# Reordering and re-splitting the work between two token groups at the start of three matmul phases (dsa_shortconv_adaln_hybrid_step)

## The reference, cut to what matters

```python
def rms_norm(x, g):
    xf = x.astype(jnp.float32)
    y = xf * lax.rsqrt(jnp.mean(xf * xf, axis=-1, keepdims=True) + EPS)
    return y.astype(x.dtype) * g
...
def swiglu(h, w_gu, w_down):
    g, u = jnp.split(h @ w_gu, 2, axis=-1)
    return (jax.nn.silu(g) * u) @ w_down
...
        hp = rms_norm(yp, norm2_g[i]) * (1.0 + sc2p) + sh2p
        hs = rms_norm(ys, norm2_g[i]) * (1.0 + sc2s) + sh2s
        yp = yp + g2p * swiglu(hp, ffn_w_gu[i], ffn_w_down[i])
```

## Time and profile before

| | us |
|---|---|
| runs of the kernel before | 2651.3, 2657.64, 2664.18 (median 2657.64) |
| profiled execution, its own time | 2652.49 |
| profiled execution, span | 2650.6 |
| PE busy | 2514.7 (95%) |
| DVE busy | 1758.2 (66%) |
| POOL busy | 1274.7 (48%) |
| ACT busy | 1125.5 (42%) |

### The profile page before, as it was taken

One profiled execution on the slowest core, in us unless ns is written; L12 is line 12 of the kernel. 1 busy time (PEld: TensorE's weight loads), 2 busy tenths in 40 slices (PEclk: granted clock), 3 DMA queues, 4 the chain that ended last, 5 costly groups with the idle time before them and its releaser, 6 DMA issues.

```text
span 2650.6 us, 51647 instructions
## 1 busy us (share of the span) xinstructions
PE 2514.7 (95%) x20164; PEld 2315.4 (87%) x20164; DVE 1758.2 (66%) x3095; ACT 1125.5 (42%) x2073; POOL 1274.7 (48%) x967
## 2 busy tenths in 40 slices
PE   6979999999998999999999989999979999999999
PEld 4848864677898999999999989999979999999999
DVE  6498888665256665657667767766675666656775
ACT  5155656775245444444212453332454444442223
POOL 3403653343143656556545435545345656654444
PEclk7999999999999999999999999999999999999999
DMA  9215557102333434344985233338324434359731
GB/s 321 77 24 161 178 205 257 52 1 86 115 111 97 155 122 155 130 154 154 343 302 196 83 97 106 106 97 324 103 76 150 155 118 159 130 201 363 285 137 70
DMA packets 316389, 407.99 MB, mean 154 GB/s; under 512 B 40816, under 2 KB 227032, under 8 KB 313338
## 3 DMA queue, kind: packets, MB, share of 16 engines
q1 hardware_dynamic: 316154, 404.75, 45.6%
HBM read 284.85 MB, written 119.85 MB: 153 GB/s over the span
## 4 chain that ended last, share of the span: by engine, by line
PE 69%; DVE 12%; DMA 6%; issue 4%; POOL 4%; ACT 2%; SPq 2%; DVEq 0%; ACTq 0%; POOLq 0%
PE PS L595 9%; PE PS L2476 9%; PE PS L2478 9%; PE PS L2477 9%; PE PS L2533 5%; PE PS L2535 5%; PE PS L2536 5%; PE PS L1841 3%; PE PS L1870 2%; PE PS L1852 2%; DMA t_scratch<-stage 2%; POOL ring L2838 2%; DMA a_scratch<-stage 2%; POOL stage L2851 1%; DVE s_all L1538 1%
## 5 line engine op out<-in xcount | busy, mean ns | idle before, releaser
L2476 PE MATMUL PS<-th,ring 128*128 128x264 f32 x2800 | 802.9, 287 | 27.9 <-DVE y L3040 9.3
L2478 PE MATMUL PS<-th,ring 128*128 128x264 f32 x2800 | 798.8, 285 | 0.0
L2477 PE MATMUL PS<-th,ring 128*128 128x264 f32 x2800 | 797.9, 285 | 0.0
L2476 PEld LDWEIGHTS PS<-th,ring 128*128 128x128 f32 x2800 | 529.8, 189 | 35.6 <-issue 31.8
L2477 PEld LDWEIGHTS PS<-th,ring 128*128 128x128 f32 x2800 | 530.2, 189 | 0.0
L2478 PEld LDWEIGHTS PS<-th,ring 128*128 128x128 f32 x2800 | 529.9, 189 | 0.0
L2838 POOL TENSOR_TENSOR ring<-wraw,ring 128x512 fp32r<-128x512 f32 x232 | 333.7, 1441 | 396.1 <-ACT ring L2628 395.5
L2838 POOL TENSOR_TENSOR ring<-sums,ring 128x512 fp32r<-128x512 f32 x216 | 320.8, 1487 | 278.0 <-ACT ring L2628 277.9
L2533 PE MATMUL PS<-th,ring 128*128 128x264 f32 x1232 | 353.1, 287 | 16.5 <-DVE zs L3149 6.9
L2535 PE MATMUL PS<-th,ring 128*128 128x264 f32 x1232 | 351.7, 285 | 0.0
L2536 PE MATMUL PS<-th,ring 128*128 128x264 f32 x1232 | 351.2, 285 | 0.0
(11 more groups left out here) (387 smaller groups left out, 5179.7 us busy)
## 6 DMA issues: line engine op xcount, KB each, us to landing
t_scratch<-stage SPq DMA_DIRECT2D x154, 528.0 KB, 3.2
th<-t_scratch SPq DMA_DIRECT2D x77, 1056.0 KB, 8.6
wraw<-in_ffn_w_gu_dram SPq DMA_DIRECT2D x96, 512.0 KB, 5.2
wraw<-in_ada_w_dram SPq DMA_DIRECT2D x80, 512.0 KB, 4.8
wraw<-in_ffn_w_down_dram SPq DMA_DIRECT2D x80, 256.0 KB, 6.0
wraw<-in_conv_w_in_dram SPq DMA_DIRECT2D x28, 512.0 KB, 5.2
y<-y_scratch SPq DMA_DIRECT2D x12, 1056.0 KB, 8.8
y_scratch<-y SPq DMA_DIRECT2D x6, 2112.0 KB, 8.1
```

The source lines that it names most:

```text
L2476: pe.matmul(out, hi, x[:, TH, k, :], start=(k == 0 and i in (1, 2, 5)), stop=False, skip_group_check=True)
L2477: pe.matmul(out, hi, x[:, TL, k, :], start=False, stop=False, skip_group_check=True)
L2478: last = pe.matmul(out, lo, x[:, TH, k, :], start=False, stop=(k == 3), skip_group_check=True)
```

## The change

1. The scale is taken in `dve_row`: one SCALAR_TENSOR_TENSOR (y times the scale, times 1/rms) in place of a TENSOR_TENSOR. `act_row` is one ACTIVATE in place of two: it adds the shift while it rounds to the high part. The value in `xf` no longer has the shift. `dve_low_row` is a SCALAR_TENSOR_TENSOR that adds the shift and takes off the high part.
2. The token sums are made of rows without shift. In sums 5 and 4 the shifts cancel. In 6 and 7 a shift stays that differs by row, so their high part is four ACTIVATEs of 264 columns (one for each row) in place of one of 1056, and their low part four SCALAR_TENSOR_TENSORs in place of one TENSOR_TENSOR.
3. Setup: the shift of the samples is stored less that of the prompt (`dve_sample_shift`, three times), and three small differences of shifts go to `vec_g`.
4. Group 0's token sums stand now in g0 and u0, and the mean and the reciprocal of group 1 stand among them. Group 0's sum 7 is rounded in g1.
5. u0 and u1 run in halves: rows 0 to 3 of both tiles, then rows 4 to 7 of both, so weight slots come free in another order. `act_c_item` is rewritten: the rows of group 1 stand between the weight splits of u0 and at the head of g1.
6. The diagonal matrix of group 1 lies in `t12` instead of `rs2`. In the Z item ahead of phases 1 and 2 the reciprocal of group 0 and its broadcast come one unit earlier.

```diff
-                if _stage == "C" and _kind in "gc":
-                    DONE[-1] = _res + 1 + _pos // 2 if _pos % 2 else None
+                if _stage == "C" and _pos % 2 == 0:
+                    DONE[-1] = None
...
-            for mi, ft in side_by_side() if fresh else itertools.product(range(2), range(KT)):
+            for mi, ft in side_by_side() if fresh else by_halves():
...
-                elif fresh and (mi, ft) == (1, 3):
+                elif (mi, ft) == (1, 3):
                     last.then_inc(c_mm, 1)
...
         def act_c_item(act, it):
 
-            step = 2 * (it.kind in "uh") + 4 * it.groups[0]
+            f, split = it.phase, lambda pos: act_split(act, PREP_AT[it.n, pos])
             if it.kind in "gc":
-                for mi in range(2):
-                    act_split(act, PREP_AT[it.n, mi])
-                    act_c_take(act, it, mi)
-                act_c_build(act, it.phase, step)
-                act_c_build(act, it.phase, step + 1)
-                for pos in (2, 3):
-                    act_split(act, PREP_AT[it.n, pos])
+                if it.groups[0]:
+                    for ft in range(4, KT):
+                        act_row(act, f, 1, ft)
+                split(0)
+                if it.groups[0]:
+                    act_high_sum(act, f, 0, 7)
+                act_c_take(act, it, 0)
+                split(1)
+                act_c_take(act, it, 1)
+                act_high_sum(act, f, it.groups[0], 6)
+                if it.groups[0] == 0:
+                    act_root(act, f, 1)
+                act_high_sum(act, f, it.groups[0], 5)
+                split(2)
+                split(3)
                 return
...
+            act_high_sum(act, f, it.groups[0], 4)
+            for pos in range(4):
+                split(pos)
+                if it.groups[0] == 0 and pos in (1, 2):
+                    act_row(act, f, 1, 2 * pos - 2)
+                    act_row(act, f, 1, 2 * pos - 1)
...
-            act.activation(row[:, 0:w], row[:, 0:w], ACT.Identity, bias=part(lay, pt, ft)[:, 0:1], scale=gsc[:, f + 1, ft, 0:1])\
-                .then_inc(n_af, 1)
-            act.wait_ge(n_af, n)
-            at = (T_AT[1], T_AT[2])[b]
-            act.activation(th[s][:, TH, at:at + 2, k, :], row.rearrange("p (h n) -> p h n", h=2), ACT.Copy).then_inc(n_hi, 1)
+            act.activation(th[s][:, TH, at:at + 2, k, :], norm_row(f, s, k, b).rearrange("p (h n) -> p h n", h=2), ACT.Identity,
+                           bias=shift_of(f, ft)).then_inc(n_hi, 1)
...
+            for k in range(4):
+                last = act.activation(th[s][:, TH, T_AT[i], k, :], sum_of(f, s, i)[:, k, :], ACT.Identity, bias=sum_shift(f, i, k))
+            last.then_inc(n_hi, 1)
...
-            dve.tensor_tensor(v[:, 0:w], y[:, ft, GS * s:GS * s + w], rstd_of(s)[:, 0:w], ALU.mult).then_inc(n_x, 1)
+            dve.scalar_tensor_tensor(out=v[:, 0:w], in0=y[:, ft, GS * s:GS * s + w], scalar=gsc[:, f + 1, ft, 0:1],
+                                     in1=rstd_of(s)[:, 0:w], op0=ALU.mult, op1=ALU.mult).then_inc(n_x, 1)
...
+            if step == 0:
+                dve_sum_ops(dve, f, 0, 5)
+                dve_sum_ops(dve, f, 0, 6)
+                dve_sum_ops(dve, f, 0, 7)
+                if f == 0:
+                    dve_sum_ops(dve, f, 0, 4)
             if step == 1:
                 dve_mean(dve, f, 1)
+                dve_low_sum(dve, f, 0, 6)
                 dve_recip(dve, f, 1)
+                if f:
+                    dve_sum_ops(dve, f, 0, 4)
...
+            if step == 5:
+                dve_sum_ops(dve, f, 1, 5)
+                dve_low_sum(dve, f, 0, 7)
+                dve_sum_ops(dve, f, 1, 6)
+                dve_sum_ops(dve, f, 1, 7)
+                dve_low_sum(dve, f, 1, 6)
```

More of the change, by code:

```diff
@@ L326, with sum_op @@
 NBLK, BLK = 6, GS // 6
-FRESH = [it.n for it in ITEMS if it.stage == "C" and it.kind in "gc"]
+C_ITEMS = [it.n for it in ITEMS if it.stage == "C"]
 T_ORD = (6, 5, 4, 7)
 def row_lo(f, s, ft):
-    return 24 * f + 8 * s + ft + 1
+    return 24 * f + 11 * s + ft + 1
 def sum_lo(f, s, i):
-    return 24 * f + 16 + 4 * s + T_ORD.index(i) + 1
-def sum_op(f, s):
-    return 8 * f + 4 * s
+    return 24 * f + (8 + T_ORD.index(i) if s == 0 and i != 7 else 19 if s == 0 else 20 + T_ORD.index(i)) + 1
+def sum_op(f, s, i):
+    return 8 * f + 4 * s + (5, 6, 7, 4).index(i) + 1
 C_END = {(it.phase, it.groups[0]): it.res + 2 for it in ITEMS if it.stage == "C"}
@@ L1340, in dve_gains_late @@
             for q in range(2, 4):
+                dve_sample_shift(dve, q)
                 dve_gsc(dve, q)
             dve.wait_ge(gsc_rdy, 4)
+            for f in range(3):
+                lay, pt = sh_sc(f + 1)
+                sh = part(lay, pt)
+                last = dve.tensor_tensor(vec_g[:, 4 * f:4 * f + 4].unsqueeze(2), sh[:, 4:8, 0:1], sh[:, 0:4, 0:1], ALU.subtract)
+            last.then_inc(gsc_rdy, 1)
+            dve.wait_ge(gsc_rdy, 5)
         TILES = list(range(2, 8))
@@ L2253, in diag_of @@
         def diag_of(f, s):
-            return hx[0:BLK, 12, 0:GS] if f == 0 and s == 0 else rs2[0:BLK, s, :]
+            if s:
+                return t12[0:BLK].rearrange("p a n -> p (a n)")
+            return hx[0:BLK, 12, 0:GS] if f == 0 else rs2[0:BLK, 0, :]
         def rstd_of(s):
@@ L2508, in pe_c_item, with by_halves @@
                 pe_stats(pe, f, 1)
+        def by_halves():
+            return [(mi, 4 * b + k) for b in range(2) for mi in range(2) for k in range(4)]
         def side_by_side():
@@ new lines, in dve_low_sum @@
+            for k in range(4):
+                last = dve.scalar_tensor_tensor(out=th[s][:, TL, T_AT[i], k, :], in0=sum_of(f, s, i)[:, k, :], scalar=sum_shift(f, i, k),
+                                                in1=hi[:, k, :], op0=ALU.add, op1=ALU.subtract)
+            last.then_inc(n_lop, 1)
+        def dve_c_build(dve, f, step):
+            row, low = lambda ft: dve_row(dve, f, 1, ft), lambda ft: dve_low_row(dve, f, 1, ft)
+            if step == 0:
[4 more added lines that the diff above has]
+                    dve_sum_ops(dve, f, 0, 4)
@@ new lines, in dve_c_build @@
+            if step == 2:
+                dve_low_sum(dve, f, 0, 5)
+                dve_low_sum(dve, f, 0, 4)
+                dve_samples(dve, f)
+                row(0)
+                row(1)
+                low(0)
+                row(2)
+            if step == 3:
+                low(1)
+                row(3)
+            if step == 4:
+                for ft in range(2, KT):
+                    low(ft)
+                    if ft < 6:
+                        row(ft + 2)
+            if step == 5:
[4 more added lines that the diff above has]
+                dve_low_sum(dve, f, 1, 6)
@@ L3126, in dve_c_item @@
+            if step == 6:
+                dve_sum_ops(dve, f, 1, 4)
+                dve_low_sum(dve, f, 1, 5)
+            if step == 7:
+                dve_low_sum(dve, f, 1, 4)
         def dve_c_item(dve, it, late):
```

118 lines of the change are left out of this document (47 added, 71 removed).

## The result

The changed kernel takes 2635.38 us (median of 8 runs, 2633.03 to 2642.85) against 2658.45 (8 runs, 2651.3 to 2667.75): a ratio of 0.9916, 95% interval 0.9897 to 0.9935, 23.1 us faster.

The account below looks back on a forecast made before the run. PE, busy 95%, was taken as the bound, so only its idle or slow time could be won. The walk's -16.4 us plus 1.5 of setup, clock counted 0, gave -15: 2643 us, range 2629 to 2657.

Parts of the forecast that it names:

- rival A: The forecast itself for the whole kernel: 10 to 20 us faster, chance 0.50.
- walk: Stepping the four engine queues through the three boundaries at full clock: 3.4, 6.8 and 6.2 us gained, 16.4 in all.
- setup: Shift instructions added on DVE ahead of an update PE waits for: 1 to 2.5 us exposed, 1.5 taken, once.
- first U item: In boundary 0, waits of 3.2 and 1.6 us replaced by one of 1.0, u1's takes being free of sums.
- ACT's row: One ACTIVATE of 0.82 us in place of two: 0.66 us less per row, 10.6 us per boundary.
- Rival D: Slower: DVE's low parts with a scalar run at half rate, +0.6 us per row, 2684 us; chance 0.06.
- The earlier rows of group 0: In boundaries 1 and 2, waits of g0 for rows shrink: 1.5 us gained in each.
- u0's broadcast: Group 1's broadcast in u0 comes late behind the pieces of sum 6: 1.6 us in boundary 0, 2.4 in boundary 1.
- The wait in u1: After 24 matmuls of u1, PE waits 4.9 us for a weight slot whose ACT split stands behind sum 5.
- The clock: Stretches at 1.2 GHz, 1.7 us each: ten before, 8 to 14 after; difference counted 0, bounds -4 to +7.
- B: Most of the gain eaten by dearer pieces, half clock behind u1 waits and setup: 2648 to 2657 us, chance 0.27.
- C: More gain, by pieces at their lower bounds and DVE rows at the old cost: 2628 to 2637 us, chance 0.17.

Follow-up runs that it names:

- takes_first: slots_by_use with takes moved ahead in the first U item and the late gains put behind the last plain update: 2618.11 us, 0.9855.
- sums_in_u1: The changed kernel with group 1's four sums put back into u1, as before the change: 2632.09 us, one run.
- split_ahead: The changed kernel with ACT splitting the third weight slot right behind the second, ahead of sums 6 and 5: 2625.22 us, one run.
- slots_by_use: The changed kernel with a C item's four weight slots numbered in PE's order of use, the first two split early: 2619.74 us, 0.9853.
- order_alone: The changed kernel with the old arithmetic put back (two ACTIVATEs per row, one-instruction sums, no shift setup): 2639.3 us, 0.9944 against the kernel before.
- one_piece: The changed kernel with sums 6 and 7 made by one instruction each in place of four, leaving out their shift: 2640.66 us, one run.

## Why the prediction was right, point by point

The forecast was 2643, and the kernel runs at 2635.4, inside the range of 2629 to 2657. The chances had faster by over 0.5% ahead of no change by only 0.48 to 0.46. The gain of 21.6 us by the boundaries lies above the 10 to 20 of rival A, which was the forecast itself. By items, forecast (walk and setup) and measured:

| phase | | g0 | u0 | g1 | u1 | first U item | sum |
|---|---|---|---|---|---|---|---|
| 0 | forecast | +1.5 | +1.3 | -2.0 | +1.2 | -3.9 | -1.9 |
| 0 | measured | +0.3 | +0.5 | -3.6 | +0.9 | -4.0 | -5.9 |
| 1 | forecast | -1.5 | +0.9 | -2.2 | -0.1 | -3.9 | -6.8 |
| 1 | measured | -1.6 | +0.4 | -3.7 | +1.4 | -2.8 | -6.3 |
| 2 | forecast | -1.5 | +1.2 | -1.9 | -0.2 | -3.8 | -6.2 |
| 2 | measured | -1.6 | +0.3 | -3.6 | -0.6 | -4.0 | -9.4 |

In all -14.9 was forecast and -21.6 measured. The largest part of the gain, in the first U item, was right in place and nearly in size.

**Durations.** Groups by form, after; they answer to the earlier trace rows:

```profile
L3083 DVE SCALAR_TENSOR_TENSOR th<-xf,mod,th 128x528 fp32r<-128x528 f32 x48 | 40.8, 858 | 4.4 <-ACT th L2795 4.0
L2795 ACT ACTIVATE th<-xf,mod 128x528 fp32r<-128x528 f32 x48 | 34.6, 735 | 21.0 <-DVE xf L3076 20.4
L3076 DVE SCALAR_TENSOR_TENSOR xf<-y,gsc,PS 128x528 f32<-128x528 f32 x24 | 17.9, 758 | 0.7 <-PE PS L2611 0.6
...
L2822 ACT ACTIVATE th<-tB,mod 128x264 fp32r<-128x264 f32 x24 | 10.4, 504 | 1.7 <-DVE tB L3104 1.4
```

DVE's row is 758 ns (765 forecast). A low row that nothing holds takes 0.75 to 0.76 (0.77 forecast; its mean of 858 has those beside POOL in it). That was in part luck: 1.25 against 1.19 ns per column, the forecast's own figures, give 0.03 at 528 columns and not the 0.06 that was added. ACT's row is 735 ns, where 819 was forecast from the form with scale and bias that writes in place: the form with a bias alone that writes the high part took 84 ns less. A piece on ACT takes 0.50 (0.59 forecast, lower bound 0.43), four of them 1.72 (2.1 forecast). On DVE a piece takes 0.48 to 0.49 (0.49 forecast), four of them 1.71 when free, and 2.7 to 3.8 beside POOL. Rival D, the half rate of a scalar instruction with two SBUF sources, was refuted by L3083. Its shortest, median and longest stand here below those of the same shape without a scalar in the kernel before:

```profile
L3056 DVE TENSOR_TENSOR th<-xf,th x48: 693/708/1717, 772.3 to 1935.8; 128x528 fp32r<-128x528 f32 x48
...
L3083 DVE SCALAR_TENSOR_TENSOR th<-xf,mod,th x48: 752/762/1284, 775.1 to 1931.4; 128x528 fp32r<-128x528 f32 x48
```

So the rule of the Trainium skill ("Vector Engine (DVE) Microarchitecture Reference", section "7. Points that are easy to get wrong") isn't borne out by this case.

**The setup** was charged at 1.5 us. DVE's block there went from 4.2 to 4.8 us, PE's wait only grew from 0.87 to 1.13, and takes_first, which moves the late gains away, won 1.4 for all of it. It was mis-sized by 1.2.

**The walk.** The U item was right, and so was its cause, at least in part: sums_in_u1 gives 6.7 of its 10.7 us back. The earlier rows of group 0 gave the 1.5 that they should. u0's broadcast wasn't late: PE has no listed wait for it in any phase, where 1.6 and 2.4 us were forecast, and ACT's pieces ahead of it were shorter. That is the 2.2 us by which u0 was too long in the forecast.

**The wait in u1** was forecast at 4.9, and came at 2.65, 3.87 and 2.62, in its place and for its cause (split_ahead, slots_by_use). By the forecast's own sign ("wrong if the u1 wait is well off 4.9") its size was wrong. The step that was off is "which waits for DVE's seventh sum": in phase 0 ACT's sum 5 started at 843.11 right behind the pieces. Where POOL holds DVE's sum 7 or 6, as in order_alone and one_piece, the wait is 3.6 to 4.5. The waits were 5.6 us too long in all, and u1 came out near the forecast all the same (+1.8 for +0.9), since the half clock behind them took about as much. That is luck: the two misses have different causes.

**The clock.** "I count 0 for the difference, with -4 to +7 as bounds." One stretch at 1.2 GHz costs 1.7 us, as forecast. The profile holds twelve times this before (20.5 us; ten were counted) and seven times after (12.0; 8 to 14 were counted), 8.5 less. But on the scale of the walk, which has the waits as they would be at full clock, not all of this is time. Where a wait follows whose end other engines set, a stretch only shortens this wait, as the prediction said of some. The windows of u1 in phases 1 and 2 of the kernel before show it, the first with a stretch at 1.2 GHz, the second with a wait of 1.33 us at its end in its place:

```profile
1567.23:1584.03 16.80, 13.51 (x99) 13.24 (x97) 14.71 (x11) 8.87 (x11) 6.17 (x4) 0.90 0.22 63
1948.87:1965.63 16.76, 12.14 (x98) 11.74 (x97) 14.67 (x11) 8.87 (x11) 6.14 (x4) 1.00 0.24 64
```

The same holds of u0 after (15.77 us at 1.00 in phase 0, 15.72 at 0.89 in phase 1). For boundary 0 the prediction has both walks, and they can be set beside the traces:

| boundary 0 | u0 | g1 | u1 | first U item | sum | half clock in the trace |
|---|---|---|---|---|---|---|
| before, walk | 15.5 | 15.7 | 15.3 | 26.4 | 72.9 | |
| before, traced | 15.3 | 17.2 | 15.3 | 26.8 | 74.6 | 6.8 |
| after, walk | 16.8 | 13.7 | 16.5 | 22.5 | 69.5 | |
| after, traced | 15.8 | 13.6 | 16.2 | 22.9 | 68.5 | 1.7 |

(g0 is left out: the walk has 12.5 for it both times, the traces 14.7 and 14.9.) Before, 6.8 us of half clock made it only 1.7 longer than the walk, nearly all in g1: of the two stretches there the first stood ahead of the weight wait, 4.1 in the walk and 2.14 in the trace. After, it is 1.0 shorter than the walk in spite of 1.7 us of half clock. So here the clock's difference was about 0, as counted, and the terms that were off are the walk's waits, 2.7 us too long (mostly 2.2 in u1 and 1.0 in u0), and the setup, 1.2 too much. That is the miss of 4.0 in this boundary. For the other two the walk's times aren't on record, so how their misses (+0.5 and -3.2) divide between clock and waits stays open.

**The rivals.** B's time was refuted; the half clock behind the u1 waits, its reason, did come (about 6 us), but the waits themselves were shorter. C's time came true (2628 to 2637), but not by its reason: neither the pieces (0.50 against its 0.43 on ACT, 0.48 against its 0.42 on DVE) nor DVE's row (758 against 696 ns) came at the low cost that it asks for, and with the pieces cut to one instruction (one_piece) the boundaries moved by 0.5 us. What the forecast never asked is what each part of the change is worth by itself. The 10.6 us per boundary that the rows save on ACT were almost all hidden: order_alone has none of them and gains 19.6.

## What to carry to other kernels

Work off an engine that isn't the bound moves the time only through what queues behind it: find that instruction first, and ask whether its place in the queue can be changed for nothing. Here the order in which weight slots are numbered, split and used was worth 16.5 us, and the shorter arithmetic 2.0 by the items (with those slots it was no gain at all). Where a matmul order is changed, the order in which buffers are filled has to change with it.

Count the clock from the windows over the whole stretch (length times one less the granted clock), and then ask of each stretch what follows it. Ahead of a wait whose end another engine sets it costs nothing (u1 took 16.80 us with a stretch and 16.76 without). Where PE has free work behind it, it costs 1.7 us here, and a kernel that loses the wait gains that too.
